# Where a recurrence's weight steps stand: 22 directly ahead of the levels of a pair in place of 8

## The chip, the cores and the metric

One core of a Trainium2 chip runs the whole kernel. The metric is device microseconds of one execution; the times stand below as the median of several runs. TensorE does the matrix products, VectorE and ScalarE the elementwise work, GpSimd (POOL) a little of it, and SyncE's queue brings in the weights.

## The reference, cut to what matters

Three layers in float32 over 256 tokens of width 2048. The first is a hybrid layer: windowed attention, a recurrence over time in both directions, and attention over a memory, gated and merged. The case touches the recurrence only:

```python
def rwkv7_scan(r, w, k, v, kk, a):
    decay = jnp.exp(-jnp.exp(w))
    b = kk * a
    def step(S, inp):
        r_t, d_t, k_t, v_t, kk_t, b_t = inp
        sa = jnp.einsum('bhij,bhj->bhi', S, -kk_t)
        S = S * d_t[:, :, None, :] + sa[..., None] * b_t[:, :, None, :] + v_t[..., None] * k_t[:, :, None, :]
        return S, jnp.einsum('bhij,bhj->bhi', S, r_t)
```

It runs for 12 heads of 64 channels, once forwards and once backwards. Beside it the layer needs projections `h @ w_in` (the gates), which do not depend on the recurrence.

## The kernel before, in words

**Weights.** All weight matrices come as one stream of tiles of 128 output channels; a tile has 16 k-steps in two units of 8. A unit (128x1024) is loaded into one of four slots of `raw`. ScalarE rounds it (`split_hi`, L316, its instruction L326: `w_hi`), VectorE makes the rest (`split_lo`, L328, L335: `w_lo`), and TensorE multiplies. A k-step of the gates' tiles is `product` (L342): three matmuls of 256 columns (L346, L347, L348), each with its weight load. `units_used` counts the units that TensorE is done with; a split of the unit four further on waits for it. A tile's result is taken from its bank by VectorE (`dve_pair_gate`, L1117, L1121), and the bank's next tile waits for that (`gate_kept`).

**The recurrence.** The 12 heads are worked in six pairs, pair 0 to pair 5, each in both directions (d = 0 and 1), the time cut into four chunks of 64. A pair's work on TensorE (`pe_rwkv`, L1415) comes in this order:

- small products zw, za, vtok at its start, then a stretch of weight k-steps, "the preparation", during which VectorE, ScalarE and POOL make the operands abd, bbd, kbd and rbd;
- "the Gram stretch": products mt, kat, m; 5 weight steps; brt, krt, btok; 4 weight steps; katv, krtv, u0, ktok; 8 weight steps; kv. Each product is a set of 64x64 matmuls recorded at L1425, and most wait for VectorE to have masked an earlier one (L1354, L1360);
- "the levels", five rounds of products X, T and U that invert a triangular matrix by doubling, each waiting for a copy or a sum of the one before; between them the hops of the previous pair's scan over chunks.

Each pair takes 64 weight k-steps (4 tiles, `BESIDE`) from the gates' projections, as filler that needs nothing of the recurrence. `go(n)` (L1131) issues the next n of them. The numbers are written by hand: `GO_START`, `GO_PREP`, `GO_GRAM` and, for the last pair, `GO_ALONE` (L92 to L94). Pairs 1 to 4 have 47 in the preparation, pair 0 has 2 at its very start and 45 in it, pair 5 has 31 and 16 spread over its own scan.

**The other engines' lists.** They are in program order too, written by hand. ScalarE's pair (L1215): tanh, exp, splits of units, the copies btok (L1242) and ktok (L1246) from the banks, `ends`, another split, then the levels' copies X (L1256). VectorE's pair (L1312): two splits, scans, gates' parts, then abd and bbd (L1336), split, ks, ksr, q (L1340 to L1344), split, gate 1, split, then the masks mt, kat, m (L1354), brt, krt (L1360), gate 2, split, the parts of katv and krtv (L1368 to L1375), u0, split, gate 3, kv, the levels. The last pair has gate 1 and the second of these splits later. "Operands turned" are btok and ktok: bbd and kbd multiplied by a stacked identity, which puts time on the partitions.

Of the kernel before, what the change touches and what calls it, by code (L numbers as in the profile page):

```python
# [19 lines left out]
KT = D // P  # L20
# [66 lines left out]
BESIDE = 1 + 3  # L87
# [1 line left out]

GO_START, GO_PREP = 2, 45  # L92
GO_ALONE = (2, 2, 1, 2, 1, 2, 2, 1, 2, 1)
GO_GRAM = (5, 4, 8)  # L94


SHIFT_OF = 2
# [100 lines left out]
def need(eng, steps, name, it=None):  # L198

    eng.wait_ge(steps.sem, steps.at(name, it))  # L200


class Tile:
# [5 lines left out]
    def sum(self, c, m):  # L209

        for reg, per in self.loops:
            c = reg * (per * m) + c
        return c
# [38 lines left out]
def build(nc, stream, consts, params, w2, a2, wgu, memT, xT, metaT, out):  # L252
# [4 lines left out]
    with ctx:  # L257
# [58 lines left out]
        def split_hi(act, tile, units=(0, 1)):  # L316

            if not tile.loops and tile.first + tile.t >= N_TILES + PAD:
                return
            for k in units:  # L320
                slot = (2 * tile.parity + k) % RING
                g = tile.first + tile.t
                act.wait_ge(raw_in[slot], tile.sum(16 * (g // 2 + 1), 8))
                if not tile.start:
                    act.wait_ge(units_used, tile.units(k + 1 - RING))
                nc.scalar.activation(w_hi[:, slot], raw[:, slot], ACT.Copy).then_inc(hi_ready, 1)  # L326
# [685 lines left out]
        def dirs_of(p):  # L1012

            return [pairs_of[2 * d + p % 2] for d in range(2)]
# [83 lines left out]
        def step_bank(p, d):  # L1098

            return banks[d] if p < PAIRS - 1 else bank_of(d, 0)  # L1100
# [10 lines left out]
        def bank_of(d, k):  # L1111
            return banks[2 + 3 * d + k]

        def pair_tile(p, j):
            return Tile(FIRST["rwkv"], j, ((p, BESIDE),))
# [33 lines left out]
        def chunks(ap):  # L1149
            return ap.rearrange("p (c t) -> p c t", c=NCH)  # L1150
# [4 lines left out]
        def value_part(bank, k):  # L1155

            return bank[:, T * k:T * k + T].rearrange("p (c i) -> p c i", c=NCH)
# [7 lines left out]
        def chunk_of(d, s):  # L1165
            return s if d == 0 else NCH - 1 - s
# [36 lines left out]
        def act_rwkv(act):  # L1203

            need(act, kk_v, "half")
            act.wait_ge(shift_step, 3 * SHIFT_T)

            def hop(p, n):
                kind, s = HOPS[n]
                if p >= 0 and kind == "SA":  # L1210
                    for d, w in enumerate(dirs_of(p)):
                        need(act, st_p, f"SA{s}_{d}", p)
                        st_a.done(nc.scalar.activation(w["nkatv"][:, chunk_of(d, s)], step_bank(p, d)[:, 0:CH], ACT.Copy), f"SA{s}_{d}")

            def pair(p, between):  # L1215
                dirs, last = dirs_of(p), p == PAIRS - 1
                nc.scalar.activation(tanh_warm[:], tanh_warm[:], ACT.Tanh).then_inc(warmed, 1)
                for d, w in enumerate(dirs):
                    need(act, rw_p, f"zw{d}", p)
                    rw_a.done(nc.scalar.activation(w["th"][:], bank_of(d, 0)[:, 0:T], ACT.Tanh, scale=0.5,  # L1220
                                                   bias=hw_sb[:, bass.ds(p + PAIRS * d, 1)]), f"thw{d}")
                    need(act, rw_p, f"za{d}", p)
                    rw_a.done(nc.scalar.activation(w["ad"][:], bank_of(d, 1)[:, 0:T], ACT.Tanh, scale=0.5,
                                                   bias=hw_sb[:, bass.ds(p + (2 + d) * PAIRS, 1)]), f"tha{d}")
                need(act, rw_p, "vtok0", p)
                rw_a.done(nc.scalar.activation(v_tok[0][:], value_part(bank_of(0, 2), 0), ACT.Copy), "vtok0")
                need(act, rw_p, "vtok1", p)
                rw_a.done(nc.scalar.activation(v_tok[1][:], value_part(bank_of(1, 2), 0), ACT.Copy), "vtok1")
                split_hi(act, pair_tile(p, 0).later(), (0,))
                for d, w in enumerate(dirs):  # L1230
                    need(act, rw_v, f"s{d}", p)
                    rw_a.done(nc.scalar.activation(w["e1"], chunks(w["s"][:]), ACT.Exp, scale=-HALF_DECAY), f"e1{d}")
                    rw_a.done(nc.scalar.activation(w["e3"][:], w["s"][:], ACT.Exp, scale=HALF_DECAY), f"e3{d}")
                split_hi(act, pair_tile(p, 0).later(), (1,))
                split_hi(act, pair_tile(p, 1).later(), (0,))
                if not last:
                    split_hi(act, pair_tile(p, 1).later(), (1,))
                    split_hi(act, pair_tile(p, 2).later(), (0,))
                for d, w in enumerate(dirs):

                    need(act, rw_p, f"btok{d}", p)
                    rw_a.done(nc.scalar.activation(w["btok"][:], value_part(bank_of(d, 2), 0), ACT.Copy), f"btok{d}")  # L1242
                split_hi(act, pair_tile(p, 1 if last else 2).later(), (1,))
                for d, w in enumerate(dirs):
                    need(act, rw_p, f"ktok{d}", p)
                    rw_a.done(nc.scalar.activation(w["ktok"][:], value_part(bank_of(d, 1), 0), ACT.Copy), f"ktok{d}")  # L1246
                for d, w in enumerate(dirs):
                    rw_a.done(nc.scalar.activation(w["ends"][:], w["end"], ACT.Copy), f"end{d}")
                split_hi(act, pair_tile(p, 2 if last else 3).later(), (0,))
                for l in LV:  # L1250
                    for d, w in enumerate(dirs):
                        need(act, rw_p, f"X{l}_{d}", p)
                        if l > 1:

                            need(act, rw_p, f"U{l - 1}_{d}", p)
                        rw_a.done(nc.scalar.activation(w["x"][:], value_part(bank_of(d, 1), 0), ACT.Copy), f"X{l}_{d}")  # L1256
                        hop(p - 1, 2 * (l - 1) + d)
                    between(f"level{l}")
                if not last:
                    split_hi(act, pair_tile(p, 3).later(), (1,))  # L1260

            for p in range(PAIRS - 1):
                pair(p, lambda place: None)
            p = PAIRS - 1
            pair(p, lambda place: act_gn_early(act, place))
            for n, (kind, s) in enumerate(HOPS):
                hop(p, n)
                if kind == "SA":
                    act_gn_early(act, f"step{s}")
                    if s == 1:  # L1270
                        split_hi(act, pair_tile(p, 2).later(), (1,))
            split_hi(act, pair_tile(p, 3).later())
            need(act, st_p, "Y_1", p)
            need(act, st_v, "Y_1", p)
# [140 lines left out]
        def pe_rwkv(pe):  # L1415
# [3 lines left out]
            for p in range(PAIRS):  # L1419
                go = pe_pair_tiles(pe, p)  # L1420
# [20 lines left out]
                istack = const("istack")  # L1441
                dirs, last_pair = dirs_of(p), p == PAIRS - 1
                w0, w1 = dirs
                if p == 0:
                    go(GO_START)

# [10 lines left out]
                both((bank_of(0, 2), 0, v_pair, istack, 0, "vtok0"), (bank_of(1, 2), 0, v_pair, istack, 1, "vtok1"))  # L1457
                if p > 1:
                    need(pe, st_v, "Y_1", p - 2)
                go(GO_PREP + (GO_START if p > 0 else 0) - (sum(GO_ALONE) if last_pair else 0))  # L1460

                for d in D2:
                    need(pe, rw_v, f"bbd{d}", p)
# [3 lines left out]
                both(*[(bank_of(d, 1), 0, w["kbd"], w["abd"], d, f"kat{d}") for d, w in enumerate(dirs)])  # L1467
                need(pe, rw_a, "vtok1", p)
                both(*[(bank_of(d, 2), 0, w["abd"], w["bbd"], d, f"m{d}") for d, w in enumerate(dirs)])
                go(GO_GRAM[0])  # L1470
                for d in D2:
                    need(pe, rw_v, f"mt{d}", p)
                    need(pe, rw_o, f"rbd{d}", p)
# [4 lines left out]
                for d in D2:  # L1478
                    need(pe, rw_v, f"m{d}", p)
                both(*[(bank_of(d, 2), 0, w["bbd"], istack, d, f"btok{d}") for d, w in enumerate(dirs)])  # L1480
                go(GO_GRAM[1])
                for d in D2:
                    need(pe, rw_v, f"krt{d}", p)

# [3 lines left out]
                need(pe, rw_a, "btok1", p)  # L1488
                both((bank_of(1, 2), 0, w1["bbd"], w1["abd"], 0, "u0_1"))
                both(*[(bank_of(d, 1), 0, w["kbd"], istack, d, f"ktok{d}") for d, w in enumerate(dirs)])  # L1490
                go(GO_GRAM[2])
                for d in D2:
                    need(pe, rw_a, f"ktok{d}", p)
                    need(pe, rw_v, f"krtv{d}", p)
# [122 lines left out]
        def act_gn_early(act, place):  # L1617

            if place == "level2":
                act_gn_hi(act, 0)  # L1620
            elif place == "level4":
                act_gn_hi(act, 1)
            elif place == "step0":
                need(act, gn_v, "center1")
                gn_a.done(nc.scalar.activation(gsq[:], y24[:, 0:EARLY], ACT.Square), "sq")
            elif place == "step1":
                act_gn_hi(act, 2)
            elif place == "step2":
                need(act, gn_v, "var1")
                gn_a.done(nc.scalar.activation(gstd[:, 0:EARLY], gvar[:, 0:EARLY], ACT.Sqrt, bias=GN_EPS, scale=1.0 / CH), "std")  # L1630
# [1889 lines left out]
```

## Time and profile before

| | |
|---|---|
| median of 3 runs | 3491.66 us (3489.72 to 3493.41) |
| profiled execution, own time | 3490.53 us |
| its span | 3488.7 us |
| TensorE busy | 3415.0 us, 98% |
| VectorE busy | 2445.8 us, 70% |
| ScalarE busy | 1640.4 us, 47% |
| GpSimd busy | 268.6 us, 8% |
| mean granted TensorE clock | 0.997 |
| pairs 0 to 5 of the recurrence | about 363 to 669 us of the span |

The rows of a timeline give start, duration, engine, line, operation, what is written and read, and a count; in square brackets the engine's idle time just before and what ended it. Times are microseconds from the start of the span. PE is TensorE, PEld its weight loads, DVE VectorE, ACT ScalarE, POOL GpSimd. "issue" is idle time for which the profile shows no wait. Matmuls overlap in the pipeline, so starts are more telling than durations.

### The profile page before, as it was taken

Reading aid. Unit: us, or ns where it says so; the run is one execution under the profiler, and the core shown is the slowest. Engines: PE = TensorE matmul, PEld = TensorE weight load, DVE = VectorE, ACT = ScalarE, POOL = GpSimd, SP = SyncE. Lnnn points to the kernel's source line nnn. Section 1 sums busy time; section 2 is a strip of 40 time slices with the busy share of each in tenths; the row PEclk is TensorE's granted clock in tenths of the full one; section 3 lists DMA queues with packets and bytes.
Section 4 is the critical chain, followed back from the end, with each engine's and each line's share of the span. In section 5 each row is a group of like instructions: output and inputs, shape, how many; then the busy total and the mean of one; then the engine's idle time right before and its main releaser. Section 6 shows DMA issues by size and latency. Waiting matters only on the chain.

```text
span 3488.7 us, 72789 instructions
## 1 busy us (share of the span) xinstructions
PE 3415.0 (98%) x27182; PEld 3094.0 (89%) x27182; DVE 2445.8 (70%) x3525; ACT 1640.4 (47%) x2261; POOL 268.6 (8%) x340
## 2 busy tenths in 40 slices
PE   8999999999999999999999999999999999999998
PEld 8999888899988899998888888888899888888886
DVE  6887777866776678877656565777766865656566
ACT  6456433444444435744435343443544644434344
POOL 5000233100010000001000000020001100000002
PEclk9999999999999999999999999999999999999999
DMA  7444322255655555555655555555545555655554
GB/s 254 163 156 136 122 81 82 90 190 188 208 190 186 181 181 177 162 176 186 193 186 193 184 192 184 188 187 192 168 159 169 169 188 185 193 180 192 187 193 138
DMA packets 164990, 604.07 MB, mean 173 GB/s; under 512 B 18336, under 2 KB 18464, under 8 KB 164560
## 3 DMA queue, kind: packets, MB, share of 16 engines
q1 hardware_dynamic: 163584, 596.16, 52.6%
q8 instruction: 134, 2.20, 0.3%
q10 hardware_dynamic: 1040, 3.16, 0.2%
q0 software_dynamic: 192, 2.23, 0.2%
q14 instruction: 40, 0.33, 0.0%
HBM read 599.38 MB, written 2.10 MB: 172 GB/s over the span
## 4 chain that ended last, share of the span: by engine, by line
PE 87%; DVE 7%; ACT 3%; issue 2%; POOL 0%; DMA 0%; ACTq 0%; DVEq 0%; POOLq 0%
PE bank L367 40%; PE bank L370 20%; PE bank L346 8%; PE bank L348 7%; PE bank L347 7%; PE bank L1425 3%; DVE w_lo L335 2%; ACT w_hi L326 1%; POOL x_norm_acc L467 0%; DVE X L3056 0%; ACT pr L774 0%; DVE X L3060 0%; ACT L774 0%; PE bank L734 0%; DVE conv_sq L2740 0%
## 5 line engine op out<-in xcount | busy, mean ns | idle before, releaser
L326 ACT ACTIVATE w_hi<-raw 128x1024 fp32r<-128x1024 f32 x1126 | 1158.6, 1054 | 829.9 <-PE bank L370 557.8
L335 DVE TENSOR_TENSOR w_lo<-raw,w_hi 128x1024 fp32r<-128x1024 f32 x1126 | 1348.6, 1234 | 113.8 <-ACT w_hi L326 113.5
L367 PE MATMUL bank<-hid,w_hi 128*128 128x512 f32 x2048 | 643.4, 395 | 0.0
L367 PE MATMUL bank<-u,w_hi 128*128 128x512 f32 x1536 | 484.4, 397 | 0.0
L370 PEld LDWEIGHTS bank<-hid,w_lo 128*128 128x128 f32 x2048 | 384.7, 188 | 90.9
L367 PE MATMUL bank<-xh,w_hi 128*128 128x512 f32 x1312 | 413.5, 397 | 2.9 <-DVE w_lo L335 2.9
L370 PE MATMUL bank<-hid,w_lo 128*128 128x256 f32 x2048 | 402.3, 278 | 0.0
L370 PEld LDWEIGHTS bank<-u,w_lo 128*128 128x128 f32 x1536 | 289.5, 189 | 69.2
L346 PE MATMUL bank<-hx,w_hi 128*128 128x256 f32 x1088 | 316.6, 291 | 12.3 <-DVE w_lo L335 11.4
L367 PEld LDWEIGHTS bank<-hid,w_hi 128*128 128x128 f32 x2048 | 311.9, 189 | 0.1
L347 PE MATMUL bank<-hx,w_hi 128*128 128x256 f32 x1088 | 308.4, 283 | 0.2 <-issue 0.2
L348 PE MATMUL bank<-hx,w_lo 128*128 128x256 f32 x1088 | 308.4, 283 | 0.0
L370 PE MATMUL bank<-u,w_lo 128*128 128x256 f32 x1536 | 302.4, 278 | 0.0
L370 PEld LDWEIGHTS bank<-xh,w_lo 128*128 128x128 f32 x1312 | 247.2, 188 | 58.5
L370 PE MATMUL bank<-xh,w_lo 128*128 128x256 f32 x1312 | 258.4, 278 | 0.0
L367 PEld LDWEIGHTS bank<-u,w_hi 128*128 128x128 f32 x1536 | 234.1, 188 | 0.1
L2464 DVE SCALAR_TENSOR_TENSOR X<-X,bank 128x256 f32 (+1 forms) x128 | 53.9, 421 | 256.5 <-PE bank L370 256.1
L346 PEld LDWEIGHTS bank<-hx,w_hi 128*128 128x128 f32 x1088 | 209.2, 192 | 19.4 <-issue 16.0
L346 PE MATMUL bank<-u,w_hi 128*128 128x272 f32 (+4 forms) x768 | 219.6, 286 | 5.9 <-DVE w_lo L335 5.9
L2396 ACT ACTIVATE ff_q<-ff_r 128x256 f32<-128x256 f32 x128 | 53.4, 418 | 353.7 <-DVE ff_r L2448 181.8
L347 PE MATMUL bank<-u,w_hi 128*128 128x272 f32 (+4 forms) x768 | 219.7, 286 | 0.0
L348 PE MATMUL bank<-u,w_lo 128*128 128x272 f32 (+4 forms) x768 | 219.6, 286 | 0.0
(480 smaller groups left out, 5964.7 us busy)
## 6 DMA issues: line engine op xcount, KB each, us to landing
raw<-stream SPq DMA_DIRECT2D x1126, 512.0 KB, 4.0
x_raw<-xT SPq DMA_DIRECT2D x4, 512.0 KB, 7.5
mem_raw<-memT ACTq DMA_DIRECT2D x4, 512.0 KB, 9.5
x_res<-xT POOLq DMA_DIRECT2D x1, 2048.0 KB, 9.2
out<-X SPq DMA_DIRECT2D x3, 512.0 KB, 2.7
cst<-consts SPq DMA_DIRECT2D x1, 1504.0 KB, 13.4
out<-X SPq DMA_DIRECT2D x2, 256.0 KB, 2.2
w_sb<-w ACTq DMA_DIRECT2D x1, 384.0 KB, 4.8
```

Source lines behind the costliest of these rows:

```text
L326: nc.scalar.activation(w_hi[:, slot], raw[:, slot], ACT.Copy).then_inc(hi_ready, 1)
L335: nc.vector.tensor_tensor(w_lo[:, slot], raw[:, slot], w_hi[:, slot].bitcast(F), ALU.subtract).then_inc(lo_ready, 1)
L346: nc.tensor.matmul(dst, w_hi[:, slot, j], hi, start=first, stop=False)
L347: nc.tensor.matmul(dst, w_hi[:, slot, j], lo, start=False, stop=False)
L348: return nc.tensor.matmul(dst, w_lo[:, slot, j], hi, start=False, stop=last)
L367: nc.tensor.matmul(bank[:], w_hi[:, slot, i], both(moving, kt), start=kt == 0, stop=False)
L370: last = nc.tensor.matmul(bank[:, T:], w_lo[:, slot, i], moving[:, kt, 0, moving.shape[-1] - T:], start=False, stop=kt == KT - 1)
L1425: last = nc.tensor.matmul(out[halves()[r ^ cross]], lhs[halves()[r]], rhs[halves()[r]], start=start, stop=stop)
L2396: nc.scalar.activation(self.q[b][:], self.r[b][:], ACT.Square).then_inc(self.sq, 1)
L2464: nc.vector.scalar_tensor_tensor(self.x[:, m], self.x[:, m], self.scale if self.is_group(g, 0) else 1.0, banks[tile.parity][:, 0:T], ALU.m ...
```

## The change

The constants: `GO_PREP` goes, and what is left of a pair's 64 steps is the preparation. Pairs 0 to 4 get 5, 4 and 22 steps in the Gram stretch, the last pair keeps 5, 4 and 8. So pairs 1 to 4 have 33 steps in the preparation (pair 0 has 31 and its 2 at the start), the last pair 31 as before. ScalarE's order changes in pairs 0 to 4: the split of unit 0 of the tile two further on moves from ahead of the btok copies to behind them, that of unit 1 from behind the btok copies to behind the ktok copies and `ends`. VectorE's and POOL's lists are untouched.

```diff
-GO_START, GO_PREP = 2, 45
+GO_START = 2
-GO_GRAM = (5, 4, 8)
+GO_GRAM, GO_GRAM_LAST = (5, 4, 22), (5, 4, 8)
...
                 if not last:
                     split_hi(act, pair_tile(p, 1).later(), (1,))
-                    split_hi(act, pair_tile(p, 2).later(), (0,))
                 for d, w in enumerate(dirs):
 
                     need(act, rw_p, f"btok{d}", p)
                     rw_a.done(nc.scalar.activation(w["btok"][:], value_part(bank_of(d, 2), 0), ACT.Copy), f"btok{d}")
-                split_hi(act, pair_tile(p, 1 if last else 2).later(), (1,))
+                split_hi(act, pair_tile(p, 1 if last else 2).later(), (1,) if last else (0,))
                 for d, w in enumerate(dirs):
                     need(act, rw_p, f"ktok{d}", p)
                     rw_a.done(nc.scalar.activation(w["ktok"][:], value_part(bank_of(d, 1), 0), ACT.Copy), f"ktok{d}")
                 for d, w in enumerate(dirs):
                     rw_a.done(nc.scalar.activation(w["ends"][:], w["end"], ACT.Copy), f"end{d}")
-                split_hi(act, pair_tile(p, 2 if last else 3).later(), (0,))
+                if last:
+                    split_hi(act, pair_tile(p, 2).later(), (0,))
+                else:
+                    split_hi(act, pair_tile(p, 2).later(), (1,))
+                    split_hi(act, pair_tile(p, 3).later(), (0,))
...
+                gram = GO_GRAM_LAST if last_pair else GO_GRAM
...
-                go(GO_PREP + (GO_START if p > 0 else 0) - (sum(GO_ALONE) if last_pair else 0))
+                go(BESIDE * KT - sum(gram) - (sum(GO_ALONE) if last_pair else 0) - (GO_START if p == 0 else 0))
...
-                go(GO_GRAM[0])
+                go(gram[0])
...
-                go(GO_GRAM[1])
+                go(gram[1])
...
-                go(GO_GRAM[2])
+                go(gram[2])
```

## Rows read from the trace of the kernel before

**Rows 1.** The page, part 4: the chain that ended last, share of the span by line

```profile
PE bank L367 40%; PE bank L370 20%; PE bank L346 8%; PE bank L348 7%; PE bank L347 7%; PE bank L1425 3%; DVE w_lo L335 2%; ACT w_hi L326 1%; POOL x_norm_acc L467 0%; DVE X L3056 0%; ACT pr L774 0%; DVE X L3060 0%; ACT L774 0%; PE bank L734 0%; DVE conv_sq L2740 0%
```

**Rows 2.** Stretches of pair 1: length; busy (count) by engine; clock; DMA; GB/s

```profile
411.10:428.20 17.10, 17.10 (x150) 16.96 (x141) 14.52 (x26) 7.80 (x13) 3.12 (x4) 1.00 0.39 132
428.20:441.10 12.90, 12.31 (x356) 11.56 (x355) 8.35 (x18) 3.40 (x8) 7.74 (x9) 1.00 0.36 115
441.10:460.30 19.20, 15.25 (x617) 13.71 (x616) 11.30 (x37) 6.12 (x20) 4.88 (x7) 1.00 0.10 31
...
447.42:451.53 4.11, 3.02 (x123) 2.76 (x123) 3.13 (x11) 1.11 (x4) 1.46 (x2) 1.00 0.02 4
```

**Rows 3.** TensorE's waits, periods of pairs 0 to 4; the instruction queue, 408 to 462

```profile
PE bank L1425 <- issue: 0.8, 2, 0.4
...
PE bank L1425 <- issue: 2.8, 5, 0.9
...
PE bank L1425 <- issue: 2.9, 5, 1.1
...
PE bank L1425 <- issue: 2.9, 5, 0.8
...
PE bank L1425 <- issue: 2.8, 3, 1.1
...
q8 instruction: 10, 0.16, 1.2%
```

**Rows 4.** TensorE's timeline, the Gram stretch of pair 1

```profile
428.24 0.69 PE L1425 MATMUL bank<-abd,bbd 64*64 64x64 f32 x32
...
431.79 0.69 PE L1425 MATMUL bank<-rbd,bbd 64*64 64x64 f32 x32
...
433.87 0.46 PE L1425 MATMUL bank<-cst,bbd 64*64 64x64 f32 x14 [0.59 <-issue]
434.25 0.38 PE L346 MATMUL bank<-hx,w_hi 128*128 128x256 f32 x1
...
441.13 0.69 PE L1425 MATMUL bank<-v_tok,ktok 64*64 64x64 f32 x32
```

**Rows 5.** VectorE's timeline, bbd and the first mask of pair 1

```profile
422.52 0.41 DVE L1336 TENSOR_TENSOR bbd<-bb,e 128x256 f32<-128x256 f32 x1
...
428.97 0.76 DVE L1354 SCALAR_TENSOR_TENSOR mt<-bank,cst 128x256 f32<-128x256 f32 x2 [1.12 <-PE bank L1425]
```

**Rows 6.** The last pair: VectorE's first mask, then TensorE's brt and next weight step

```profile
626.56 0.75 DVE L1354 SCALAR_TENSOR_TENSOR mt<-bank,cst 128x256 f32<-128x256 f32 x2
...
627.56 0.69 PE L1425 MATMUL bank<-rbd,bbd 64*64 64x64 f32 x32 [0.62 <-DVE mt L1354]
...
629.40 0.39 PE L346 MATMUL bank<-hx,w_hi 128*128 128x256 f32 x1
```

**Rows 7.** The same mask and brt in pairs 0 and 4, VectorE's and TensorE's timelines

```profile
381.79 0.76 DVE L1354 SCALAR_TENSOR_TENSOR mt<-bank,cst 128x256 f32<-128x256 f32 x2 [0.95 <-PE bank L1425]
...
384.60 0.69 PE L1425 MATMUL bank<-rbd,bbd 64*64 64x64 f32 x32
...
579.80 0.76 DVE L1354 SCALAR_TENSOR_TENSOR mt<-bank,cst 128x256 f32<-128x256 f32 x2 [1.11 <-PE bank L1425]
...
582.62 0.69 PE L1425 MATMUL bank<-rbd,bbd 64*64 64x64 f32 x32
```

**Rows 8.** Stretches around two holes of TensorE elsewhere, columns as in rows 2

```profile
1448.00:1451.00 3.00, 0.92 (x7) 0.92 (x8) 2.00 (x4) 2.71 (x6) 0.00 (x0) 1.00 0.51 173
1451.00:1455.00 4.00, 4.00 (x23) 4.00 (x22) 3.96 (x6) 3.56 (x7) 0.00 (x0) 0.57 0.40 133
...
1490.00:1493.00 3.00, 0.87 (x7) 0.66 (x7) 2.97 (x6) 0.42 (x1) 0.00 (x0) 1.00 0.03 12
1493.00:1497.00 4.00, 3.66 (x31) 3.45 (x31) 2.99 (x4) 2.32 (x3) 0.00 (x0) 1.00 0.41 131
```

## The prediction

> **What bounds the kernel now.** TensorE carries the chain of waits that ended last; in it the weight products of the long phases stand first and the 64x64 products of the recurrence (L1425) have 3% [rows 1]. So nearly every microsecond that TensorE gains or loses inside a pair is one of the kernel's, and only that stage has to be read. I read it in this order: the busy time by stretches, TensorE's timeline, VectorE's timeline, the waits.
>
> In pair 1 (the second of six) the stretch of 47 weight k-steps takes 17.10 us, the Gram stretch (six small products, 17 weight steps among them) 12.90 us, the levels 19.20 us [rows 2]. TensorE is busy throughout in the first, nearly so in the second (12.31), and 15.25 us in the levels. A weight k-step is 17.10 / 47 = 0.36 us.
>
> The levels' holes are largely not waits for data. The waits put down to "issue" come to 0.8, 2.8, 2.9, 2.9 and 2.8 us in the periods of pairs 0 to 4 [rows 3]. From 447.42 to 451.53 us the engine runs 123 matmuls and 123 weight loads, and some waits, in 4.11 us [rows 2]; the instruction queue moved ten packets of 16 KB in the 54 us around this pair [rows 3]. So I read a block of some 250 instructions every 4.1 us as the pace at which TensorE's code arrives.
>
> **The change, part by part.** *Counts.* The 64 weight steps of a pair stay 64. In pairs 0 to 4 the preparation gets 14 fewer and the stretch directly ahead of the products kv gets 22 in place of 8; the last pair has its old numbers. Nothing is added on an engine or a queue: no DMA, no matmul, no copy.
>
> *Weight steps taken out of the preparation.* 14 x 0.36 = 5.0 us a pair. Can what follows start 5.0 us earlier? In pair 1 product mt starts at 428.24 [rows 4]; 33 steps instead of 47 would bring it to 423.2. Its operand bbd is finished by VectorE at 422.52 + 0.41 = 422.93 [rows 5]: just in time, cost nothing. Its products then run, then five weight steps as before. Product brt is next, and it needs mt masked by VectorE. VectorE's list is not changed: after bbd it makes a split, three products of its own, a split, a gate and a split, and only then comes to mt. That list ends where its wait before mt begins: 428.97 - 1.12 = 427.85 [rows 5]. Before, TensorE was later than VectorE there; now VectorE is later. It can mask mt from 427.85 only.
>
> How long from there to brt? The last pair shows exactly this regime, having only 31 steps of preparation: VectorE begins mt at 626.56 and TensorE begins brt at 627.56, after a wait for it [rows 6]. So brt follows by 1.00 us. For pair 1: 428.85, against 431.79 before [rows 4]: 2.94 us earlier, not 5.0. Pair 0: VectorE free at 381.79 - 0.95 = 380.84, brt 381.84 against 384.60: 2.76. Pair 4: free at 578.69, brt 579.69 against 582.62: 2.93 [rows 7]. Pairs 2 and 3 repeat pair 1. Sum over five pairs: 2.76 + 2.94 + 3 x 2.93 = 14.5 us gained up to brt, while 5 x 5.04 = 25.2 us of weight steps are put back behind it. **Net +10.7 us.**
>
> *From brt to the next weight steps.* Before, brt, krt and btok take about 1.56 us (pair 1 has a code stall in it: 431.79 to 434.25 with 0.59 of "issue") [rows 4]. With VectorE's masks only just ahead it is 627.56 to 629.40 = 1.84 us in the last pair [rows 6]. I take 0.28 us more per pair, **+1.4 us**. Bounds: nothing (masks in time) and 5 x 0.6 if krt and btok each wait a full pair of masks.
>
> *ScalarE's order.* The btok copies now stand ahead of the hi split of the tile two further on (unit 0), the ktok copies ahead of that of unit 1. This has to be, since those splits now wait for weight steps that TensorE issues behind btok and ktok. Cost nothing: the copies wait for TensorE alone, the splits are wanted only in the next pair or late in this one, and the first activation behind them (X of level 1) comes after kv. The cover is the 22 steps: TensorE passes the sixth of them 2.2 us in, the fourteenth 5.0 us in, and a split takes about 1 us, so the last hi is done some 2 us before kv. Without that cover X of level 1 would be late by up to 1 us.
>
> *VectorE behind krt.* Gate 2 now waits until tile 2 has ended, six steps into the 22, and the katv, krtv and u0 work queues behind it. TensorE needs krtv only after all 22. By steps of its list (gate 0.3, split 1.2, five operations at 0.33) VectorE is done some 3.2 us after the sixth step, TensorE takes 16 x 0.36 = 5.8 us: 2.6 us to spare. Nothing; if that cover went (a slow split), tenths.
>
> *Code blocks.* kv stands at the same place in TensorE's instruction stream as before, so the levels meet the block borders at the same instructions, and their pace of a block in 4.1 us is unchanged: levels +0. In the Gram stretch the borders move by 84 instructions (14 steps of six). In pair 1 the stall of 0.59 us [rows 4] falls away, because the border before it is now followed by the wait for mt. In the others I find between nothing and 0.3 us either way. **-0.5 us**, bounds -2 and +1.5.
>
> Sum: 10.7 + 1.4 - 0.5 = **+11.6 us**. The profiled execution took 3490.53 us, the median of the runs is 3491.66, 1.1 above it; the sum is added to the median: 3503.3 us.
>
> **A rule that speaks the other way.** The trace gives TensorE 17 us of preparation with some 290 instructions [rows 2], time for four blocks at 4.1 us, and then 12.9 + 19.2 us in which it uses about 710 and 1230. Yet it stalls for code already at 433.87 [rows 4], so it does not enter the Gram stretch with a large store. The Trainium skill, "Runtime: NRT & Kernel Launch", section "Instruction fetch mechanics", gives TensorE 128 KiB of instruction memory, a FIFO of 2048 instructions refilled in blocks of 256. By that rule 22 slow steps ahead of the levels would let code pile up, and the levels would run free of it. The trace agrees with the block size; it speaks against the depth. The same section, a few lines on, says that the memory is only two lines and that the prefetch is purely sequential, which is what the rows look like.
>
> **The rivals.**
> 1. *Code runs ahead in the 22 steps (faster side).* Place: TensorE's stalls at block borders in the levels. Price: all of the issue waits of the five periods, 0.8 + 2.8 + 2.9 + 2.9 + 2.8 = 12.2 us [rows 3], and what the levels win behind them. With those alone it comes to 11.6 - 12.2 = -0.6: 3491. It decides from 2.3 us a pair; to be faster by over 0.2% it needs 3.7 us a pair, the levels shrinking from 19.2 to 15.5, near their busy 15.25 [rows 2]: some 3483 us. For: a long slow stretch stands directly ahead. Against: the 17 us of preparation bring no such store. Chance 0.22, half of it with a gain of over 0.2%.
> 2. *The clock falls in the new hole.* TensorE would stand idle from about 426.6 to 428.85 in pair 1, 2.2 us. Elsewhere a hole of that size (0.92 busy of 3.00 us) was followed by a granted clock of 0.57 over 4 us, that is in part at 1.2 instead of 2.4 GHz; another (0.87 busy) was followed by 1.00 [rows 8]. At 0.57 for 4 us some 1.7 us are lost; in all five pairs 8.6: 3512 us. Against: the Gram products stand on both sides and the rows split evenly. Chance 0.1.
> 3. *VectorE is not that late.* If VectorE's list is shorter once its splits and gates find everything ready, or brt follows the masks at 0.5 us instead of 1.0, each pair pays 1.0 to 1.4 instead of 2.3: +5 to +7, 3497 to 3499. Chance 0.1.
> That the change does not do what it says is excluded by the sums in the code: 33 + 5 + 4 + 22 = 64.
>
> **How the numbers follow.** The forecast has the rest, 0.58, with its own range of 3499 to 3508 from the bounds above. A difference of 0.2%, about 7 us, is what a measurement of this kernel can tell from no change. Faster by more: half of rival 1, 0.11. Within: the other half of rival 1, most of rival 3 and a tail of the forecast, 0.2. Slower: 0.69. The range leaves out the gain of rival 1 and the worst of rival 2: 3491 to 3509.
>
> **What would show it.** After: the wait of TensorE for mt about 2.2 us in pairs 0 to 4 (now none there), VectorE with no wait before mt, and mt on VectorE 0.95 to 1.12 us earlier than now relative to the pair's start. The wait for bbd near nothing. From brt to the weight steps about 1.84 us. Levels 19.2 us in pair 1 as before, with issue waits near 3 us. The pair's period longer by 1.6 to 2.6 us. I am wrong if the levels shrink by over 1 us a pair, if brt starts 5 us earlier, or if the granted clock falls under 1.00 in the pairs.

## The result, and the profile after

The changed kernel takes 3503.29 us (median of 7 runs, 3501.96 to 3505.51), the kernel before 3491.05 us (7 runs, 3487.28 to 3493.41): ratio 1.0038, 95% interval 1.0028 to 1.0048. It is slower by 12.2 us. The prediction had 3503.3 us and +11.6.

Stretches of the changed kernel: pair 1 (the preparation, the Gram stretch with its 22 steps, the levels), pair 2 (the Gram stretch, the levels), and as the last row 3.4 us of pair 1 that begin 0.8 us behind the start of brt; columns as in rows 2:

```profile
413.90:426.00 12.10, 12.10 (x111) 11.94 (x101) 9.93 (x20) 5.86 (x13) 3.13 (x4) 1.00 0.39 131
426.00:446.80 20.80, 18.78 (x398) 17.94 (x397) 12.29 (x25) 5.61 (x10) 7.30 (x9) 0.92 0.34 105
446.80:465.10 18.30, 15.18 (x617) 13.71 (x616) 11.31 (x37) 6.13 (x20) 4.33 (x6) 1.00 0.09 30
478.90:498.00 19.10, 17.14 (x398) 16.48 (x397) 12.25 (x25) 5.58 (x10) 7.31 (x9) 1.00 0.36 115
498.00:518.00 20.00, 15.50 (x618) 13.97 (x616) 11.20 (x37) 6.13 (x20) 4.33 (x6) 1.00 0.09 29
432.40:435.80 3.40, 3.40 (x72) 3.28 (x66) 1.62 (x5) 0.69 (x3) 3.28 (x5) 0.51 0.50 154
```

Against [rows 2] the preparation of pair 1 is 5.0 us shorter (17.10 to 12.10), the Gram stretch 7.9 us longer (12.90 to 20.80). Of these 7.9, 5.0 are the 14 weight steps; TensorE stands idle for 2.0 us of the stretch, against 0.6 before.

TensorE's timeline of the changed kernel, products mt and brt of pair 1, and brt of pair 2:

```profile
426.05 0.69 PE L1428 MATMUL bank<-abd,bbd 64*64 64x64 f32 x32
...
431.63 0.59 PE L1428 MATMUL bank<-rbd,bbd 64*64 64x64 f32 x25 [1.96 <-DVE mt L1357]
...
484.48 0.69 PE L1428 MATMUL bank<-rbd,bbd 64*64 64x64 f32 x32 [1.96 <-DVE mt L1357]
```

VectorE's timeline over the same stretch of pair 1:

```profile
425.37 0.41 DVE L1339 TENSOR_TENSOR bbd<-bb,e 128x256 f32<-128x256 f32 x1
425.71 1.21 DVE L335 TENSOR_TENSOR w_lo<-raw,w_hi 128x1024 fp32r<-128x1024 f32 x1
426.84 0.41 DVE L1343 TENSOR_TENSOR kd<-kd,kd 128x256 f32<-128x256 f32 x1
427.29 0.35 DVE L1345 TENSOR_SCALAR kd<-kd,par 128x256 f32<-128x256 f32 x1
427.68 0.43 DVE L1347 TENSOR_TENSOR rkv<-rkv,kd 128x256 f32<-128x256 f32 x1
428.02 1.22 DVE L335 TENSOR_TENSOR w_lo<-raw,w_hi 128x1024 fp32r<-128x1024 f32 x1
429.16 0.42 DVE L1121 TENSOR_TENSOR gate<-bank,x_norm_rstd 128x256 f32<-128x256 f32 x1
429.49 1.21 DVE L335 TENSOR_TENSOR w_lo<-raw,w_hi 128x1024 fp32r<-128x1024 f32 x1
430.62 0.75 DVE L1357 SCALAR_TENSOR_TENSOR mt<-bank,cst 128x256 f32<-128x256 f32 x2
```

In [rows 5] VectorE waited 1.12 us for TensorE ahead of the mask of mt. Now it goes from bbd to the mask without a gap, and TensorE waits for it: brt starts 1.01 us behind the mask, after 1.96 us of waiting, where in [rows 4] it started unhindered. The wait appears once in each of pairs 0 to 4, with 1.96 us in pairs 1 to 4 and 2.08 us in pair 0. TensorE's waits from 361 to 700 us, first two rows of the changed kernel's answer (before, the wait for mt was 0.6 us, once, in the last pair):

```profile
PE bank L1428 <- issue: 13.7, 25, 1.6
PE bank L1428 <- DVE mt L1357: 10.6, 6, 2.1
```

### The profile page after: what moved, and what is told of

Its sections match the earlier page's. It is cut to its first block, busy times and chain, and to the rows that moved or that the text cites. A ratio compares the mean times of both kernels' runs of the same rounds, so it can differ in the third digit from the quotient of the medians.

```text
span 3501.5 us, 72789 instructions
## 1 busy us (share of the span) xinstructions
PE 3419.8 (98%) x27182; PEld 3097.9 (88%) x27182; DVE 2442.5 (70%) x3525; ACT 1641.4 (47%) x2261; POOL 264.0 (8%) x340
## 4 chain that ended last, share of the span: by engine, by line
PE 85%; DVE 9%; ACT 4%; issue 2%; POOL 0%; DMA 0%; ACTq 0%; DVEq 0%; POOLq 0%
PE bank L367 40%; PE bank L370 20%; PE bank L346 7%; PE bank L348 7%; PE bank L347 7%; PE bank L1428 3%; DVE w_lo L335 3%; ACT w_hi L326 1%; POOL x_norm_acc L467 0%; DVE X L3060 0%; ACT pr L774 0%; DVE bb L1331 0%; DVE X L3064 0%; ACT L774 0%; DVE bbd L1339 0%
## 5 line engine op out<-in xcount | busy, mean ns | idle before, releaser
L346 PE MATMUL bank<-hx,w_hi 128*128 128x256 f32 x1088 | 317.8, 292 | 11.6 <-DVE w_lo L335 10.6
```

Source lines behind the costliest of these rows:

```text
L346: nc.tensor.matmul(dst, w_hi[:, slot, j], hi, start=first, stop=False)
```

## The experiments

Each was timed 11 times beside the kernel before on the same chip, in three groups; below stand the medians. The kernel before stood at 3488.51 us beside the kernels with 15 and 19 steps, the filled hole and the masks first; at 3488.37 us beside ScalarE's order, the shift by a whole block, the masks first with 16 steps and the last pair with 22; at 3490.49 us beside the other three. "Levels" is the time from kv to the next pair's first product, summed over pairs 0 to 4 of one profile: 92.5 us in the kernel before, 90.7 in the changed one.

**How many steps can be moved: 7 and 11 in place of 14.** Against the changed kernel:

```diff
-GO_GRAM, GO_GRAM_LAST = (5, 4, 22), (5, 4, 8)
+GO_GRAM, GO_GRAM_LAST = (5, 4, 15), (5, 4, 8)
```

> 15 weight steps directly ahead of the levels in place of 22, so 7 fewer in the preparation than the kernel before has. Theory (TensorE waits for VectorE's first mask, which is free 0.95 to 1.12 us before it is needed in the kernel before, so brt cannot start more than 2.9 us earlier): 7 x 0.36 = 2.5 us is under 2.9, so TensorE does not wait for the mask, and the time is that of the kernel before, within +2 us (the masks just ahead of krt and btok). Rival (weight steps directly ahead of the levels cost or win by themselves): half of the 12.2 us lost, about +6, or a win that grows with the steps.

Measured: 3490.22 us, ratio 1.0005 (0.9996 to 1.0014). No wait for the mask in pairs 0 to 4; brt starts 3.55 us behind mt as before.

With 19 in place of 15:

> 19 weight steps directly ahead of the levels, 11 fewer in the preparation. Theory: 11 x 0.36 = 3.96 us are moved, brt can come 2.93 earlier, so each of five pairs waits 1.0 us for the mask and pays 0.3 for krt and btok: +5 to +7 us, about 3497, and the clock does not fall, the hole being 1 us. Rival (the loss is in proportion to the steps moved): 12.2 x 11/14 = +9.6.

Measured: 3495.25 us, ratio 1.0018 (1.0009 to 1.0027), +6.7 us, inside the 5 to 7. First two rows of TensorE's waits, 361 to 620 us, of this kernel:

```profile
PE bank L1428 <- issue: 12.0, 19, 1.6
PE bank L1428 <- DVE mt L1357: 4.6, 5, 1.0
```

Five waits of 0.9 to 1.0 us, and the granted clock behind them is 1.00. So 7 steps cost nothing that can be measured, 11 cost 6.7 us, 14 cost 12.2: the loss starts at a point between 7 and 11 steps, and the theory puts it at 2.93 / 0.36 = 8.

**Filling the hole.** The short preparation stays, six of the steps go ahead of brt.

```diff
-GO_GRAM, GO_GRAM_LAST = (5, 4, 22), (5, 4, 8)
+GO_GRAM, GO_GRAM_LAST = (11, 4, 16), (5, 4, 8)
```

> The preparation as in the changed kernel (33 steps), but 11 steps ahead of brt, 4, and 16 ahead of the levels: the hole before brt is filled with 6 weight steps (2.2 us). Theory: no wait for the mask, no fall of the clock; the whole loss goes except 0.3 us a pair for krt and btok: 3491 to 3493. Rival (the shortened preparation costs by itself, through code or splits): stays at 3500 or above.

Measured: 3490.04 us, ratio 1.0002 (0.9993 to 1.0011). No wait for mt is left; brt to the next weight steps is 1.71 us in pairs 1 to 4 and 1.83 in pair 0 (1.84 in the changed kernel's pair 2, 1.56 before). The shortened preparation is not what costs; the idle TensorE is.

**Emptying VectorE's list ahead of the mask.**

```diff
-                split_lo(v, pair_tile(p, 1).later(), (0,))
-                if not ending:
-                    dve_pair_gate(v, p, 1)
-                    split_lo(v, pair_tile(p, 1).later(), (1,))
+                if ending:
+                    split_lo(v, pair_tile(p, 1).later(), (0,))
...
                 else:
+                    split_lo(v, pair_tile(p, 1).later(), (0,))
+                    dve_pair_gate(v, p, 1)
+                    split_lo(v, pair_tile(p, 1).later(), (1,))
                     dve_pair_gate(v, p, 2)
```

> The changed kernel with VectorE's list altered in pairs 0 to 4: the splits of tile 1's successor and gate 1 (1.14 + 0.34 + 1.14 = 2.6 us) stand behind the masks of krt instead of ahead of the mask of mt. 22 steps stay directly ahead of the levels. Theory: VectorE is free 2.6 us earlier, brt comes after its five weight steps with no wait, the holes and the falls of the clock go: the time returns to that of the kernel before, 3490 to 3493. If 22 steps ahead of the levels win something by themselves (code running ahead), it shows here as a time under 3488. If the place of the steps costs by itself, it stays above 3497.

Measured: 3486.98 us, ratio 0.9994 (0.9985 to 1.0003). All 22 steps stand directly ahead of the levels and none of the 12 us is lost. VectorE's timeline of pair 1 here:

```profile
424.81 0.75 DVE L1355 SCALAR_TENSOR_TENSOR mt<-bank,cst 128x256 f32<-128x256 f32 x2
...
427.12 0.76 DVE L1361 TENSOR_TENSOR brt<-bank,cst 128x256 f32<-128x256 f32 x2 [0.24 <-PE bank L1429]
```

TensorE waits for no mask in pairs 0 to 4, and ahead of the mask of brt VectorE is again the one that waits. The 3488 us named in the expectation was meant against 3491 for the kernel before; against the 3488.5 measured beside it the kernel is 1.5 us ahead, and its interval does not exclude no change.

**Moving only a part of that list.** Here the first split stays ahead of the masks, gate 1 and the second split (1.47 us) go behind them:

```diff
+                split_lo(v, pair_tile(p, 1).later(), (0,))
...
                 else:
-                    split_lo(v, pair_tile(p, 1).later(), (0,))
                     dve_pair_gate(v, p, 1)
                     split_lo(v, pair_tile(p, 1).later(), (1,))
```

> The changed kernel with gate 1 and only the second split behind the masks (0.34 + 1.14 = 1.47 us), the first split ahead of them as before. Theory: VectorE is free 1.47 us earlier than in the changed kernel, which has 2.1 us of waiting for the mask in excess of the kernel before, so 0.6 us of wait and the 0.3 us for krt and btok stay in each of five pairs: +3 to +5 us against the kernel before, and no fall of the clock in the pairs. Rival (any hole, or the place of the steps, decides and not its length): either the full 12 us or nothing.

Measured: 3492.10 us beside 3490.49, ratio 1.0005 (0.9996 to 1.0014): +1.6 us, under the 3 to 5 expected. The parts are as worked out: mt to brt takes 4.1 to 4.2 us (3.55 before), 0.6 us a pair, and brt to the next steps 1.84; together that is 4.3 us, and the granted clock stays at 1.00 behind these holes. The interval, -1.4 to +4.9 us, holds both this sum and nothing. So the rival's "full 12 us" is excluded, its "nothing" only by the waits in the profile and not by the time.

**ScalarE's order alone**, with (5, 4, 8):

> The changed kernel with the step counts of the kernel before (5, 4, 8): ScalarE's new order alone. Theory: the copies and the splits wait for TensorE and nobody waits for them, so the time is that of the kernel before, within 2 us. Rival (the order carries part of the loss): +3 us or more.

Measured: 3488.61 us, ratio 1.0001 (0.9992 to 1.0010). It costs nothing.

**Are the levels' holes waits for code?**

```diff
+                if p == 0:
+                    go(16)
+                    need(pe, rw_a, "tha1", 0)
+                    for _ in range(32):
+                        heads2(bank_of(0, 0)[:, 0:CH], istack, istack)
+                    go(GO_PREP - 16)
```

> The kernel before with 64 matmuls of 64x64 (128 instructions, weight loads counted) added once, in the preparation of pair 0, writing a bank that is overwritten later. Nothing else changes, but every later instruction of TensorE stands 128 further on, half a block of 256. Theory (TensorE's holes in the levels are waits for code, one at each block border): the products cost about 1 us once, and in pairs 1 to 4 the holes of 0.5 to 1.2 us stand about 128 instructions, some 2 us, earlier or later in the levels than in the kernel before, their number and sum about the same (12 us of issue waits); the total within 3 us of the kernel before. Rival (the holes belong to the products that wait for copies or sums): they stay at the same products.

Measured: 3493.06 us, ratio 1.0013 (1.0004 to 1.0022), +4.7 us where at most 3 were expected: the inserted products alone took 3.95 us and not about 1. This one told nothing of the borders: each product stands twice in the trace, so everything moved by 256 instructions, exactly one block, and under either theory the holes should stay where they were. In pair 1 they did at three of four places, and the first was gone. With `range(16)`:

> As the shift experiment, with 32 small products in place of 64. In the trace each of these float32 products stands as two weight loads and two matmuls, so the earlier 64 moved everything by 256 instructions, one whole block, and left the borders where they were; 32 move it by 128, half a block. Theory (holes in the levels are waits for code at block borders): in pairs 1 to 4 they stand at other products than before, half a block away: in pair 1 the borders fall 58, 314, 570 instructions behind the first kv in place of 186, 442, 698. Rival (the holes belong to certain products): they stay where they were. Time: +1 to +3 us from the products themselves, plus or minus 2 from the new places.

Measured: 3494.42 us beside 3490.49, ratio 1.0013 (1.0004 to 1.0023), +3.9 us. I counted TensorE's instructions in the trace (matmuls, weight loads and those of its sequencer) from the first kv of pair 1 to the end of each hole. Before: 442, 698, 954 and 1210, each 256 behind the last. With the half block in front: 313, 826, 1081 and 1337, 256 or 512 apart and 128 off the old places, to within one instruction; at 58 and 570, which the expectation names too, no hole stands. Pairs 2 to 4 do the same: 387, 643, 899 and 1155 in pair 2 before, 515, 771 and 1027 with the half block. The wait for the copy X of level 1 (0.37 us) stayed at its product. Holes of pair 1 in the kernel before, and of this kernel, as their timelines give them:

```profile
447.46 0.33 PE L1425 MATMUL bank<-u,x 64*64 64x64 f32 x3 [0.92 <-issue]
...
451.57 0.27 PE L1425 MATMUL bank<-tm,ml 64*64 64x64 f32 x2 [1.01 <-DVE u L1389]
...
455.38 0.27 PE L1425 MATMUL bank<-x,u 64*64 64x64 f32 x2 [0.58 <-issue]
...
459.47 0.27 PE L1425 MATMUL bank<-kv,rbd 64*64 64x64 f32 x2 [0.56 <-issue]
```

```profile
447.19 0.50 PE L1425 MATMUL bank<-u,x 64*64 64x64 f32 x10 [0.78 <-issue]
...
458.38 0.56 PE L1425 MATMUL bank<-u,x 64*64 64x64 f32 x13 [0.40 <-issue]
...
463.40 0.34 PE L1425 MATMUL bank<-cst,rkv 64*64 64x64 f32 x8 [0.79 <-issue]
```

The last hole has moved out of the levels into the next pair's vtok. The hole at 451.57 is put down to VectorE, yet it stands at a border, and with the half block no wait stands at its product. So the holes go with the place in the instruction stream, every 256 instructions, and not with the products. That they wait for code the instruction queue shows: in the kernel before one 16 KB packet goes with each of the four holes, from 445.11, 449.00, 452.92 and 457.08 us on, and each ends 1.2 to 1.5 us before TensorE goes on.

**Do 22 steps win anything?** The masks-first kernel with 16 steps:

> VectorE's masks ahead of its splits, as in the last experiment of the first call, with 16 steps directly ahead of the levels in place of 22 and 6 more in the preparation. Theory without any gain of the steps: the same time as with 22, within 1 us, a little under the kernel before. If code runs ahead in the 22 steps and is worth something in the levels, the levels of the five pairs together are 1 us or more longer than with 22 (90.9 us there, 92.5 us in the kernel before).

Measured: 3485.21 us, ratio 0.9993 (0.9984 to 1.0002). Its levels are 91.1 us, those with 22 steps 90.9, and those with 8 steps (ScalarE's order alone) 91.0. One profile says little to the microsecond: the four kernels with 8 steps ahead of the levels have 90.3 to 92.5 us, the four with 15 or 16 have 90.7 to 91.7, the five with 19 or 22 have 90.6 to 91.7. Within this spread six to fourteen more slow steps leave the levels as they are.

**The last pair too**, with its first split also behind the masks, 22 steps and then 16:

```diff
-                if ending:
-                    split_lo(v, pair_tile(p, 1).later(), (0,))
...
                 if ending:
-                    split_lo(v, pair_tile(p, 1).later(), (1,))
+                    split_lo(v, pair_tile(p, 1).later())
```

> The masks ahead of the splits with 22 steps, and the last pair too: there the split of unit 0 of tile 1's successor (1.14 us) goes behind the masks. Theory: the last pair's wait for its first mask (0.6 us) and the tight masks behind it (0.3 us) go, about 1 us less than the masks-first kernel: 2 to 3 us under the kernel before, the smallest time of this study. Rival: the last pair's splits come late for its weight steps and eat it: no gain.

> Masks ahead of the splits in all six pairs, 16 steps directly ahead of the levels. Theory: the same as with 22 steps (ratio 0.9992), between 3484 and 3487 with the kernel before at 3488.4. A gain of the 22 steps would show as 1 us or more above that.

Measured: 3485.33 us, ratio 0.9992 (0.9983 to 1.0001), and 3487.77 us beside 3490.49, ratio 0.9991 (0.9982 to 1.0000). In the last pair mt to brt falls from 4.23 to 3.54 us and brt to the weight steps from 1.84 to 1.56: the 1 us is there in the profile, and too small for the timing. Four kernels with the masks ahead of the splits stand between 0.9991 and 0.9994, 1.5 to 3.2 us under the kernel before, each with an interval that ends at or just above 1. They are probably a little faster; a single one of them doesn't show it. The masks first with the old 8 steps was not run, so whether such a gain would be that of VectorE's order alone is not shown.

## Why the prediction was right

**The mask is the bound.** Right, and to the tenth. From the first weight step of the preparation to brt pair 1 takes 17.64 us now and 20.64 before: 3.0 us gained, where 2.94 was worked out and 5.04 would have been the whole shift. Over five pairs it is 14.6 us (14.5 predicted) against 25.2 us put back. The two ways of taking the wait away (steps into it, VectorE's list behind it) both bring the whole loss back, and the doses of 7 and 11 steps fall where the sum puts them.

**brt to the next steps.** Right: 1.84 us in pairs 0, 2 and 4, 1.56 before without a stall. In pairs 1 and 3 it is 2.4 us, with the low clock in it.

**ScalarE's order, VectorE behind krt, bbd just in time.** Right: no new wait of TensorE for any of them in pairs 0 to 4; the one for X of level 1 is 0.37 us as before (0.48 in pair 0). mt starts 12.05 us behind the first step in pair 2, 33 steps of 0.36 us and 0.2.

**Code.** The sum of -0.5 us came out near -0.8, but not as I had it. I expected the levels unchanged and small stalls to cancel in the Gram stretch. In the profile pairs 0 and 4 stall 1.0 and 1.3 us more between katv and the weight steps, the stalls of pairs 0 and 1 between brt and katv (0.4 and 0.9 us) are gone, and the levels are 1.8 us shorter, by pair between 1.1 us shorter (pair 4) and 0.7 us longer (pair 2). Nothing shows the shorter levels to be the work of the change: they are 91.0 us with (5, 4, 8) and the new order on ScalarE, too. Why one profile of the kernel before has 92.5 is open; the pace of single blocks varies from 3.5 to 4.4 us in that profile.

**The clock.** Rival 2 came in part. Of the five new holes two, in pairs 1 and 3, were followed by a low clock (pair 1: 3.4 us at a granted 0.51, that is about 1.2 GHz), and three were not (pair 2: 1.00 throughout). From brt to katv pair 1 took 4.77 us and pair 2 3.46, 1.3 us more for it, and pair 3 as well: +2.6 us in this profile that the forecast's sum did not hold. The rival had 1.7 us a hole. The holes of about 1 us and less in the experiments (pairs 0 to 4 with 19 steps, and with gate 1 and one split behind the masks) were followed by full clock.

**Adding up.** For the five pairs: +25.2 of steps, -14.6 up to brt, +1.4 for the tight masks, +2.6 of clock, -0.8 of code, together +13.8 us in the profile; the two spans differ by 12.8 and the medians by 12.2. So the predicted 3503.3 is closer than the sum deserves, and that it was met to 0.1 us is luck: a clock term of 2.6 us was missing, about 1 us came back outside the pairs, and the medians differ by 0.6 us less than the two profiles.

**Its own signs.** Of the three signs of being wrong one came: the granted clock fell under 1.00 in pairs 1 and 3. One came in a single pair: the levels of pair 4 shrank by 1.1 us, those of all five by 0.4 on average. The third did not: brt came 3.0 us earlier and not 5. The pairs' periods grew by 2.0 to 3.2 us, where 1.6 to 2.6 was written. So the mechanism of the mask stands, and what was left out of the sum is the clock.

**Rival 1** is refuted: it needed 2.3 us a pair, and with 8 to 22 slow steps ahead the levels stay within the 2.2 us, over five pairs, by which single profiles differ. What the rows showed before, that 17 us of preparation build up no large store of code, holds for 8 us directly ahead too. In pairs 1 to 4 of the 13 profiles the first border behind kv passes without a hole; holes of up to 1.6 us stand at the second or third, with 8 steps and with 22 alike. The Trainium skill's depth of 2048 instructions for TensorE ("Runtime: NRT & Kernel Launch", "Instruction fetch mechanics") does not describe this kernel; its block of 256 does, and was seen to the instruction. **Rival 3** did not happen: brt followed the mask by 1.01 us.

## What to carry to other kernels

Filler work that is moved from one stretch to a later one is only free if everything behind the shortened stretch can come earlier by as much: look for the other engine's idle time just ahead of its hand-over (here 0.95 to 1.12 us, plus the 1.8 us of steps between), because that is the most that can be moved. Beyond it each step costs its full time, and in this kernel holes of 2 us were also followed by a fall of the clock in two of five cases. If more is wanted, first put what that engine does for later (splits, gates) behind what is waited for now. And a hole that looks like latency may be code arriving: if holes stand every 256 instructions, more filler ahead of them does not help.

## What the runs showed of the hardware

TensorE's largest holes in the dense stretches of 64x64 products stand at block borders of 256 instructions, and from hole to hole a block takes 3.5 to 4.4 us in the kernel before (4.1 in pair 1: 447.46 to 451.57). A hole of 1.96 to 2.08 us in TensorE was followed by a fall of the clock in two of five cases. And the inserted products, 128 recorded matmuls into one 64-column strip, took 3.95 us, 31 ns each, where the Gram products, 32 into four strips of two banks, start 16 ns apart (mt to kat in pair 2 of the changed kernel: 478.90 to 479.42). Whether the strip, the bank or the operands make the difference was not tested.
